# Delta layer of a streaming encoder step: VectorE's scan work moved between its places, transfers issued in the scan, output norms applied on ScalarE

## The chip, the cores and the metric

The kernel runs on one core of one Trainium2 chip. The metric is device time in microseconds (us). Before the change it is 1423.12 us, the median of 3 runs (1422.04 to 1426.44).

## What is computed

One inference step of two layers on 1024 prompt tokens and 8 sample sequences of 16 tokens, model width 1024. Layer 0 (a gated linear recurrence beside window attention) is untouched. Layer 1 is a gated delta rule with 8 heads of 128 channels. For each head, cut to what matters (the kernel works in chunks of 128 tokens, 8 for the prompt, and takes the 8 samples together as a ninth):

```python
v_new = u_i - w_i @ state                       # per chunk i, in order
o_i   = (q_i * exp(g_i)) @ state + qk_i @ v_new
state = state * exp(g_last) + (k_i * exp(g_last - g_i)).T @ v_new
...
o = rms_norm(o, head_norm) * silu(z)
y = o @ w_out
```

Ahead of it q, k and v come from a projection, a causal convolution of four taps, a SiLU and (q, k) an l2 norm.

## The kernel before

The code is written engine by engine; semaphores order the engines, and each engine runs its own list in order. All data are float32.

Layer 1 is a loop over heads `h`. A head has a part `rest` (the inverse of the unit lower triangular matrix of each chunk, made of many 32x32 products in rounds `r`, and the gram matrices) and a part `scan` of eight steps `k`, one for each chunk. Then three last places (`TAIL + 1` to `TAIL + 3`) lead to the next head.

TensorE has two jobs. The chain of the scan is short, and between its products TensorE makes the projection of head `h + 1`. This is cut into 112 matmuls 288 wide, spread by `SLOTS` over numbered places `p`, two to three for each; `fill(h, p, ahead)` issues a place's share. Scan step `k` has the places 12+3k, 13+3k and 14+3k. One step of the scan on TensorE is: two products with the state `SP` (`ks_mm`, which needs `st_ready`, and `qs_mm`, which needs `o_ready`), fill; a product with `RR` (`tr_mm`, which needs `r_ready`), fill; two products with `VN` (`kv_mm`, `o_mm`), fill. A projection uses sums of weight blocks, which GpSimd makes (`head_sums`: three additions of 128x512, then `last_sum`: one), since each pair of column blocks is multiplied in seven half products rather than eight.

VectorE, in each step, makes `RR`, copies `VN`, updates `SP` and adds `OO[:, k]` (one output chunk). `between(h, p, ahead)` gives each place its share of other work for head `h + 1`: the additions of half products (`added_half`), and one convolution tap (`tap`, placed by `TAP`). `exponents` prepares three chunks of the decay matrix `EE` at a time from a row that a DMA broadcasts (`rows`); `silu` finishes a convolved row; `normed` multiplies output chunks by the reciprocal norms `fo`, which GpSimd makes (`norms`); `outputs` then takes their transposes from TensorE. A 128x1024 addition updates the sample states `SS1` in step 5.

ScalarE, in each step, scales `QE`, squares `OO[:, k]`, and does the first taps and the tanh of the SiLU (placed by `TANH`). `exponent` takes the exponential of `EE`.

SyncE issues all DMAs from one queue, in order (`head` in its block): the sample states in (`SS1`) and out, weights (`weights`, 512 KB for each of four column blocks `m`), short histories of the convolution (`history`, three transfers with pieces of 12 bytes), the row for `EE` (`rows`), and the gate row of the head before (`y_dram`). `head_sums(h + 1, 1)` is the first thing in GpSimd's `scan` and needs the weights `m` = 3 and 2 of head `h + 1`; `head_sums(h + 2, 0)` follows `compact`, which needs the exponential.

Of the kernel before, what the change touches and what calls it, by code (L numbers as in the profile page):

```python
# [18 lines left out]
ALU = mybir.AluOpType  # L19
# [144 lines left out]
def closed(p):  # L164
# [9 lines left out]
       24: (QUERY, 0, 1), 25: (QUERY, 0, 2), 26: (QUERY, 0, 3), 27: (QUERY, 1, 1), 28: (QUERY, 1, 2), 29: (QUERY, 1, 3),  # L174
       36: (VALUE, 0, 1), 37: (VALUE, 0, 2), 38: (VALUE, 0, 3)}
LAST_TAP = {0: (VALUE, 1, 1), 1: (VALUE, 1, 2), 2: (VALUE, 1, 3)}
TANH = {25: KEY, 31: QUERY}
# [73 lines left out]
def encoder(nc, I, O):  # L251
    ctx = ExitStack()
    with ctx:  # L253
# [184 lines left out]
        def _(sp):  # L438
# [176 lines left out]
            def head(h, ahead):  # L615
                if h:
                    sp.wait_ge(sem("ss_out"), 16 * h)
                sp.dma_start(SS1, I["gs"][bass.ds(h, 1)].rearrange("a p s v -> p (a s) v")
                             ).then_inc(sem("ss_in"), 16)
                if 1 <= h <= H - 2:  # L620
                    sp.wait_ge(sem("y1_done"), 3 * h)
                    sp.wait_ge(sem("row_kept"), 16 * (h - 1))
                    sp.dma_start(y_dram[h - 1], YT[:, gate_row(h - 1)]).then_inc(sem("row_kept"), 16)
                if not ahead:
                    for k in range(3, KT):
                        if k in (3, 5, 7):
                            sp.wait_ge(sem("s1_ready"), 3 * H + (k - 7) // 2)
                        sp.dma_start(w1out[k], I["wout"][1, :, k]
                                     ).then_inc(sem("wout1_in" if k < KT - 1 else "wout_in"), 16)
                    sp.wait_ge(sem("hist1"), 6 * H)  # L630
                    sp.dma_start(O["cb1"], CB1).then_inc(sem("out1"), 16)
                if ahead:
                    if h:
# [15 lines left out]
                if h == H - 2:  # L649
                    sp.wait_ge(sem("row_kept"), 16 * (H - 2))  # L650
                    for i, step in enumerate(("6", "7", "5")):
                        sp.wait_ge(sem("st_mm"), passed(h + 1, 1, step))
                        for k in (2 * i, 2 * i + 1):
# [3 lines left out]
                             ).then_inc(sem("ss_out"), 16)  # L657
                if h == H - 2:
# [5 lines left out]

            for h in range(H - 2):
# [925 lines left out]
        def _(act):  # L1591
# [333 lines left out]

            def scan(h, ahead):
                for k in range(8):
# [74 lines left out]
        def _(dve):  # L2002
# [532 lines left out]
            def silu(h, m):  # L2535
# [3 lines left out]
                dve.scalar_tensor_tensor(S1[:, m, 0:SEQ], T[:, 0:SEQ], 1.0, CV[:, m, 0:SEQ],  # L2539
                                         ALU.add, ALU.mult)  # L2540
# [65 lines left out]
            def norm_q(h):  # L2606
# [5 lines left out]
                c.sync()  # L2612
# [380 lines left out]
```

## Time and profile before

| | |
|---|---|
| median of 3 runs | 1423.12 us |
| profiled execution, its own time | 1421.56 us |
| its span, first to last instruction | 1419.7 us |
| PE busy | 1367.3 us, 96% |
| DVE busy | 818.0 us, 58% |
| ACT busy | 419.7 us, 30% |
| POOL busy | 262.1 us, 18% |
| mean granted TensorE clock | 0.996 |

PE is TensorE (PEld its weight loads), DVE VectorE, ACT ScalarE, POOL GpSimd, SP SyncE; SPq is SyncE's queue of issues. The times of matmuls overlap, and their ends are modelled, so a busy PE can still lose time between two starts. Idle time is given in brackets with what ended it. L923 is the helper line of all matmuls, L926 of all transposes. A float32 matmul shows as two instructions. Layer 1's heads take the span from about 600 to 1350 us, one head about 90 us; the rows below show mostly the fifth head, whose scan runs from about 1023 to 1067 us. Scan steps take 5 to 6 us each.

### The profile page before, as it was taken

The page shows a single profiled execution, that of the slowest core. Times are in us where ns is not written, and L with a number is a line of the kernel's source. Part 1 is how long each engine was busy: PE and PEld are TensorE (multiplying, and loading weights), DVE is VectorE, ACT ScalarE, POOL GpSimd, SP SyncE. Part 2 cuts the span into 40 slices and gives each one's busy share as a digit, 9 for nine tenths or more (in the row PEclk, how much of TensorE's full clock was granted, in tenths as well). Part 3 has the DMA queues.
Part 4 walks back from the last instruction along what each step waited for, and adds up shares of the span by engine and source line. Part 5 has one row for each costly group of instructions (what it writes and reads, how often), then busy time and mean ns, then how long its engine had stood idle before and what let it go on. Part 6 is the DMA issues. An engine that isn't in the chain of part 4 may idle for free.

```text
span 1419.7 us, 30686 instructions
## 1 busy us (share of the span) xinstructions
PE 1367.3 (96%) x12976; PEld 934.0 (66%) x12976; DVE 818.0 (58%) x1851; ACT 419.7 (30%) x990; POOL 262.1 (18%) x402
## 2 busy tenths in 40 slices
PE   5999999999999999999999999999999999999998
PEld 3577765666653455567777777777778778765543
DVE  3747872444432343775867748658577585772244
ACT  4214441444420322422323223233132331322111
POOL 1113200000000112332412223123231232210111
PEclk9999999999999999999999999999999999999999
DMA  9520107000056301211120211201112111240133
GB/s 370 226 46 28 37 7 318 1 1 1 10 231 229 112 30 60 59 48 19 63 67 30 80 20 50 79 31 51 50 45 72 42 50 50 97 165 2 47 119 118
DMA packets 56316, 112.16 MB, mean 79 GB/s; under 512 B 34698, under 2 KB 37586, under 8 KB 53346
## 3 DMA queue, kind: packets, MB, share of 16 engines
q1 hardware_dynamic: 56180, 110.21, 22.2%
q8 instruction: 102, 1.67, 0.5%
q14 instruction: 34, 0.28, 0.1%
HBM read 91.79 MB, written 18.40 MB: 78 GB/s over the span
## 4 chain that ended last, share of the span: by engine, by line
PE 65%; DVE 3%; issue 2%; ACT 0%; DVEq 0%; POOLq 0%; POOL 0%; ACTq 0%
PE psum L923 63%; PE psum L926 2%; DVE mem L2515 1%; DVE mem L2702 0%; DVE mem L2553 0%; DVE mem L2486 0%; DVE mem L2720 0%; DVE mem L2752 0%; DVE mem L2404 0%; DVE mem L2765 0%; DVE mem L2401 0%; DVE mem L2843 0%; DVE mem L2603 0%; DVEq L253 0%; DVE mem L2744 0%
## 5 line engine op out<-in xcount | busy, mean ns | idle before, releaser
L923 PE MATMUL psum<-mem 32*32 32x32 f32 (+11 forms) x12368 | 1306.7, 290 | 31.6 <-issue 14.0
L923 PEld LDWEIGHTS psum<-mem 32*32 32x32 f32 (+5 forms) x12368 | 865.2, 138 | 437.9 <-issue 236.5
L2515 DVE SCALAR_TENSOR_TENSOR mem<-mem 128x576 f32<-128x576 f32 (+1 forms) x126 | 104.2, 827 | 0.0
L926 PE MATMUL psum<-mem 128*128 128x128 f32 (+1 forms) x608 | 85.7, 278 | 15.1 <-ACT mem L1613 10.7
L926 PEld LDWEIGHTS psum<-mem 128*128 128x128 f32 (+1 forms) x608 | 71.2, 144 | 41.3 <-issue 25.6
L754 POOL TENSOR_SCALAR mem<-mem 128x1 f32<-128x1 f32 x17 | 3.7, 215 | 343.8 <-ACT mem L1756 343.8
L1920 ACT ACTIVATE mem<-mem 128x128 f32<-128x128 f32 x72 | 22.0, 305 | 136.1 <-DVE mem L2752 82.9
L2357 DVE SCALAR_TENSOR_TENSOR mem<-psum,mem 128x1024 f32<-128x1024 f32 x12 | 15.2, 1270 | 60.4 <-POOL mem L756 60.4
L1735 ACT ACTIVATE mem<-mem 128x256 f32<-128x256 f32 x72 | 35.5, 494 | 46.4 <-DVE mem L2317 46.4
L1756 ACT ACTIVATE mem<-psum 128x1024 f32<-128x1024 f32 x12 | 12.3, 1025 | 110.8 <-PE psum L923 109.1
L2057 DVE TENSOR_SCALAR mem<-psum,mem 128x128 f32<-128x128 f32 x64 | 21.1, 402 | 39.1 <-PE psum L926 39.1
L1818 ACT ACTIVATE mem<-mem 128x576 f32<-128x576 f32 (+1 forms) x42 | 32.7, 779 | 28.1 <-DVE mem L2493 28.1
L1808 ACT ACTIVATE mem<-psum 128x288 f32<-128x288 f32 x28 | 11.5, 411 | 98.2 <-PE psum L923 98.2
L2307 DVE CUSTOM_DVE_ANT_0 mem<-psum,mem 128x256 f32<-128x256 f32 x72 | 25.6, 421 | 23.7 <-PE psum L923 23.7
L795 POOL TENSOR_TENSOR mem<-mem 128x512 f32<-128x512 f32 x14 | 15.3, 1091 | 119.7 <-issue 115.2
L821 POOL COPY mem<-mem 128x3 f32<-128x3 f32 x24 | 8.4, 350 | 151.7 <-DVE mem L2473 71.2
L2539 DVE SCALAR_TENSOR_TENSOR mem<-mem 128x1024 f32<-128x1024 f32 x24 | 34.9, 1453 | 1.8 <-ACT mem L1847 1.7
L2720 DVE SCALAR_TENSOR_TENSOR mem<-psum,mem 128x128 f32<-128x128 f32 x56 | 19.4, 347 | 27.1 <-PE psum L923 27.1
L1890 ACT ACTIVATE mem<-psum 128x288 f32<-128x288 f32 x32 | 13.1, 411 | 66.6 <-PE psum L923 66.5
L2731 DVE COPY mem<-psum 128x128 f32<-128x128 f32 x64 | 18.6, 290 | 23.4 <-PE psum L923 23.3
L1847 ACT ACTIVATE mem<-mem 128x1176 f32<-128x1176 f32 x24 | 28.2, 1175 | 7.0 <-DVE mem L2404 4.0
L1930 ACT ACTIVATE mem<-psum,mem 128x128 f32<-128x128 f32 x56 | 20.2, 360 | 33.2 <-PE psum L923 33.2
(242 smaller groups left out, 1175.5 us busy)
## 6 DMA issues: line engine op xcount, KB each, us to landing
mem<-modw SPq DMA_DIRECT2D x12, 2048.0 KB, 13.2
mem<-w SPq DMA_DIRECT2D x44, 512.0 KB, 4.0
mem<-x SPq DMA_DIRECT2D x1, 4608.0 KB, 17.9
x_dram<-mem SPq DMA_DIRECT2D x9, 512.0 KB, 2.6
mem<-row_dram SPq DMA_DIRECT2D x8, 576.0 KB, 4.4
mem<-x_dram SPq DMA_DIRECT2D x9, 512.0 KB, 3.6
mem<-wout SPq DMA_DIRECT2D x4, 1024.0 KB, 8.4
mem<-gs SPq DMA_DIRECT2D x8, 512.0 KB, 3.8
```

The source lines that it names most:

```text
L923: return pe.matmul(*a, **k)
L926: return pe.transpose(out, in_, ident[0:n, 0:n])
L1735: c.mark(act.activation(SS[:, a], SS[:, a], ACT.Exp, scale=HD ** -0.5, bias=nm[:, a:a + 1], accum_out=den[:, a:a + 1]))
L1818: act.activation(CV[:, m, lo:hi], U1[:, m, lo:hi], ACT.Copy, scale=CW[:, 3 * g + ORDER[m], 0:1]).then_inc(sem("pj_ev"), 1)
L1847: act.activation(U1[:, m, PRE:], CV[:, m, 0:UC], ACT.Tanh, scale=0.5).then_inc(sem("th1"), 1)
L1920: x = act.activation(SQJ, OO[:, k], ACT.Square, accum_out=sso[:, k:k + 1])
L1930: act.activation(QE, B(7)[:, 0:P], ACT.Copy, scale=HC[:, 0, k:k + 1]).then_inc(sem("qe_ready"), 1)
L2057: i = dve.tensor_scalar(HT[:, k, bass.ds(t * P, P)], src[k], modT[:, KT + k, 0:1], modT[:, k, 0:1], ALU.mult, ALU.add)
L2307: i = dve.tensor_tensor_reduce(SS[:, n], B(bk)[:, a * 256:(a + 1) * 256], mask, 1.0, -3.0e38, ALU.add, ALU.max, mx[:, n:n + 1])
L2515: x = dve.scalar_tensor_tensor(cvm, U1[:, m, lo + j:hi + j], CW[:, 3 * g + ORDER[m], j:j + 1], cvm, ALU.mult, ALU.add)
L2539: dve.scalar_tensor_tensor(S1[:, m, 0:SEQ], T[:, 0:SEQ], 1.0, CV[:, m, 0:SEQ], ALU.add, ALU.mult)
L2720: dve.scalar_tensor_tensor(RR, at_(6, 0), HC[:, 1, k:k + 1], VB[:, k], ALU.mult, ALU.add).then_inc(sem("r_ready"), 1)
```

## The change

- `TANH` and `TAP`: the tanh of the key row moves from place 25 to 24, of the query row from 31 to 32; two taps of the query row move from places 28 and 29 to 29 and 31.
- The addition to `SS1` moves from step 5 (after `OO`) to step 6 (ahead of `VN`).
- `exponents` run in steps 2, 3 and 4, not in 3, 4 and 5.
- The key row's `silu` is cut in two: columns 0 to 511 in step 5, the rest in step 7.
- `normed` leaves VectorE. ScalarE scales each of the nine chunks of `OO` by its own column of `fo`, with one instruction each: four and one in step 5, four after place `TAIL + 1`.
- SyncE: a head's first transfers wait for the first state of the scan (`st_ready` of 8h + 1). Then come `history`, the weights `m` = 2 and 3, `rows` and the gate row to `y_dram`. Before, the gate row and these weights were issued in `rest` round 1, and `history` and `rows` in its later rounds. The next `SS1` is fetched as soon as the last one has been written out. The last head waits the same way, and sends the last block of the output weights after that wait.

```diff
-       24: (QUERY, 0, 1), 25: (QUERY, 0, 2), 26: (QUERY, 0, 3), 27: (QUERY, 1, 1), 28: (QUERY, 1, 2), 29: (QUERY, 1, 3),
+       24: (QUERY, 0, 1), 25: (QUERY, 0, 2), 26: (QUERY, 0, 3), 27: (QUERY, 1, 1), 29: (QUERY, 1, 2), 31: (QUERY, 1, 3),
...
-TANH = {25: KEY, 31: QUERY}
+TANH = {24: KEY, 32: QUERY}
...
             def head(h, ahead):
-                if h:
-                    sp.wait_ge(sem("ss_out"), 16 * h)
...
-                if 1 <= h <= H - 2:
-                    sp.wait_ge(sem("y1_done"), 3 * h)
-                    sp.wait_ge(sem("row_kept"), 16 * (h - 1))
-                    sp.dma_start(y_dram[h - 1], YT[:, gate_row(h - 1)]).then_inc(sem("row_kept"), 16)
                 if not ahead:
-                    for k in range(3, KT):
+                    for k in range(3, KT - 1):
...
+                sp.wait_ge(sem("st_ready"), 8 * h + 1)
...
                 if ahead:
+                    sp.wait_ge(sem("s1_ready"), 3 * h + 3)
+                    history(h + 1)
                     if h:
                         sp.wait_ge(sem("st_mm"), passed(h, 1, "3"))
                         weights(h + 1, 2)
                     else:
                         sp.wait_ge(sem("pj_mm"), 12)
                     weights(h + 1, 3)
-                    sp.wait_ge(sem("s1_ready"), 3 * h + 3)
-                    history(h + 1)
                     sp.wait_ge(sem("eq_ready"), 3 * h + 3)
                     rows(h + 1)
+                    if h:
+                        sp.wait_ge(sem("y1_done"), 3 * h)
+                        sp.wait_ge(sem("row_kept"), 16 * (h - 1))
+                        sp.dma_start(y_dram[h - 1], YT[:, gate_row(h - 1)]).then_inc(sem("row_kept"), 16)
...
                 sp.dma_start(O["ss"][bass.ds(h, 1)].rearrange("a p s v -> p (a s) v"), SS1
                              ).then_inc(sem("ss_out"), 16)
+                if ahead:
+                    sp.wait_ge(sem("ss_out"), 16 * (h + 1))
+                    states(h + 1)
...
+            def normed(h, n, a, b):
+
+                wait(act, sem("fo_ready"), 3 * h + n + 1)
+                for k in range(a, b):
+                    i = act.activation(OO[:, k], OO[:, k], ACT.Copy, scale=fo[:, k:k + 1])
+                i.then_inc(sem("on_ready"), 1)
...
-                    if k == 5 and ahead:
-                        exponent(h + 1)
+                    if k == 5:
+                        normed(h, 0, 0, 4)
+                        if ahead:
+                            exponent(h + 1)
+                        normed(h, 1, 8, 9)
...
                     between(h, TAIL + p, ahead)
+                    if p == 1:
+                        normed(h, 2, 4, 8)
...
-            def normed(h, n, a, b):
-
-                dve.wait_ge(sem("fo_ready"), 3 * h + n + 1)
-                dve.tensor_tensor(OO[:, a:b], OO[:, a:b], bc(fo[:, a:b], 2, P), ALU.mult
-                                  ).then_inc(sem("on_ready"), 1)
...
+                        if k == 6:
+                            dve.wait_ge(sem("sample_mm"), 4 * h + SAMPLE_MM["kv"])
+                            dve.wait_ge(sem("ss_dec"), h + 1)
+                            ss = SS1.rearrange("p (b s) v -> p b (s v)", b=4)
+                            dve.tensor_tensor(ss, ss, psum[:, 2:6, 0:256], ALU.add).then_inc(sem("sample_dve"), 1)
                     dve.wait_ge(sem("tr_mm"), 8 * h + k + 1)
                     dve.tensor_copy(VN, at_(6, 1)).then_inc(sem("vn_ready"), 1)
...
+                    elif k == 5 and ahead:
+                        silu_front(h + 1, KEY, 0, LW)
                     elif k == 7 and ahead:
-                        silu(h + 1, 0)
+                        silu(h + 1, KEY, LW)
...
-                    elif k == 5:
...
-                        dve.tensor_tensor(ss, ss, psum[:, 2:6, 0:256], ALU.add).then_inc(sem("sample_dve"), 1)
-                        between(h, 14 + 3 * k, ahead)
-                        dve.wait_ge(sem("o_ready"), 8 * h + 4)
-                        normed(h, 0, 0, 4)
-                        dve.wait_ge(sem("sample_dve"), 5 * h + SAMPLE_DVE["o"])
-                        normed(h, 1, 8, 9)
...
-                    if ahead and k in (3, 4, 5):
-                        exponents(h + 1, 3 * (k - 3), 3 * (k - 2))
+                    if ahead and k in (2, 3, 4):
+                        exponents(h + 1, 3 * (k - 2), 3 * (k - 1))
```

## Rows read from the trace of the kernel before

**Rows 1.** The page's first part: busy us (share of the span) xinstructions.

```profile
PE 1367.3 (96%) x12976; PEld 934.0 (66%) x12976; DVE 818.0 (58%) x1851; ACT 419.7 (30%) x990; POOL 262.1 (18%) x402
```

**Rows 2.** TensorE's waits from 690 to 1300 us: total, times, longest.

```profile
PE psum L923 <- issue: 13.4, 11, 2.5
PE psum L923 <- DVE mem L2720: 8.7, 7, 1.2
```

**Rows 3.** Timeline of TensorE, fifth head's scan: start us, us, instructions merged.

```profile
1050.67 6.46 PE L923 MATMUL psum<-mem 128*128 128x288 f32 x31
1058.37 1.95 PE L923 MATMUL psum<-mem 128*128 128x128 f32 x8 [1.24 <-DVE mem L2720]
...
1037.05 0.85 PE L923 MATMUL psum<-mem 128*128 128x288 f32 x5
```

**Rows 4.** Timeline of VectorE, same scan, step 5 and the start of 6.

```profile
1054.13 1.21 DVE L2765 TENSOR_TENSOR mem<-mem,psum 128x1024 f32<-128x1024 f32 x1
...
1056.38 0.88 DVE L2702 TENSOR_TENSOR mem<-mem 128x512 f32<-128x512 f32 x2
1057.19 0.87 DVE L2553 SCALAR_TENSOR_TENSOR mem<-mem 128x128 f32<-128x128 f32 x3
1057.98 0.34 DVE L2720 SCALAR_TENSOR_TENSOR mem<-psum,mem 128x128 f32<-128x128 f32 x1
```

**Rows 5.** Timeline of VectorE, same scan: first state, then step 2.

```profile
1026.17 0.28 DVE L2749 COPY mem<-psum 128x128 f32<-128x128 f32 x1
...
1033.57 0.81 DVE L2515 SCALAR_TENSOR_TENSOR mem<-mem 128x576 f32<-128x576 f32 x1
...
1034.94 0.42 DVE L2736 TENSOR_TENSOR mem<-mem 128x256 f32<-128x256 f32 x1
...
1035.96 0.81 DVE L2515 SCALAR_TENSOR_TENSOR mem<-mem 128x576 f32<-128x576 f32 x1
1036.69 0.34 DVE L2744 SCALAR_TENSOR_TENSOR mem<-mem,psum 128x128 f32<-128x128 f32 x1
...
1037.87 0.34 DVE L2720 SCALAR_TENSOR_TENSOR mem<-psum,mem 128x128 f32<-128x128 f32 x1
```

**Rows 6.** Timeline of VectorE: one SiLU instruction beside GpSimd's addition, one alone.

```profile
1002.85 2.15 DVE L2539 SCALAR_TENSOR_TENSOR mem<-mem 128x1024 f32<-128x1024 f32 x1
...
1067.29 1.22 DVE L2539 SCALAR_TENSOR_TENSOR mem<-mem 128x1024 f32<-128x1024 f32 x1
```

**Rows 7.** Timeline of GpSimd, fifth head.

```profile
1002.83 1.09 POOL L795 TENSOR_TENSOR mem<-mem 128x512 f32<-128x512 f32 x1 [17.51 <-issue]
...
1017.67 1.27 POOL L784 TENSOR_TENSOR mem<-mem 128x512 f32<-128x512 f32 x1 [2.20 <-PE psum L923]
...
1059.38 1.81 POOL L809 COPY mem<-mem 32x288 f32<-32x288 f32 x4 [9.67 <-ACT mem L1852]
```

**Rows 8.** Timeline of SyncE's queue: start and us of the issues.

```profile
1005.23 1.63 SPq L583 DMA_DIRECT2D mem<-cs  x3
...
897.48 0.33 SPq L623 DMA_DIRECT2D y_dram<-mem  x1
```

**Rows 9.** DMA issues from 1083 to 1090 us: KB each, median us to landing.

```profile
mem<-w SPq DMA_DIRECT2D x2, 512.0 KB, 3.6
```

**Rows 10.** Timeline of TensorE in `rest`: stops that no semaphore ended.

```profile
902.42 2.05 PE L923 MATMUL psum<-mem 32*32 32x64 f32 x20 [2.51 <-issue]
...
810.26 1.12 PE L923 MATMUL psum<-mem 128*128 128x288 f32 x2 [1.88 <-issue]
...
1076.59 1.78 PE L923 MATMUL psum<-mem 32*32 32x32 f32 x23 [0.78 <-issue]
```

**Rows 11.** Windows: us, busy us of each engine, PEclk, DMA share, GB/s.

```profile
902.40:905.90 3.50, 3.48 (x24) 2.59 (x24) 1.45 (x5) 0.00 (x0) 0.00 (x0) 0.51 0.02 5
810.30:813.70 3.40, 3.40 (x12) 2.82 (x12) 1.21 (x2) 0.00 (x0) 0.00 (x0) 0.50 0.39 116
```

**Rows 12.** ScalarE scaling 128x128 by a column: ns min/median/max.

```profile
L1943 ACT ACTIVATE mem<-mem x64: 384/389/396, 667.2 to 1308.3; 128x128 f32<-128x128 f32 x64
```

More of the change, by code:

```diff
@@ L613, in _, with states, head @@
                 weights(1, ORDER[i])
-            def head(h, ahead):
-                if h:
-                    sp.wait_ge(sem("ss_out"), 16 * h)
+            def states(h):
                 sp.dma_start(SS1, I["gs"][bass.ds(h, 1)].rearrange("a p s v -> p (a s) v")
                              ).then_inc(sem("ss_in"), 16)
-                if 1 <= h <= H - 2:
-                    sp.wait_ge(sem("y1_done"), 3 * h)
-                    sp.wait_ge(sem("row_kept"), 16 * (h - 1))
-                    sp.dma_start(y_dram[h - 1], YT[:, gate_row(h - 1)]).then_inc(sem("row_kept"), 16)
+            def head(h, ahead):
                 if not ahead:
-                    for k in range(3, KT):
[L626 to L629, printed above, removed]
+                    for k in range(3, KT - 1):
+                        sp.wait_ge(sem("s1_ready"), 3 * H - 2 if k < 5 else 3 * H - 1)
+                        sp.dma_start(w1out[k], I["wout"][1, :, k]).then_inc(sem("wout1_in"), 16)
+                sp.wait_ge(sem("st_ready"), 8 * h + 1)
+                if not ahead:
+                    sp.wait_ge(sem("s1_ready"), 3 * H)
+                    sp.dma_start(w1out[KT - 1], I["wout"][1, :, KT - 1]).then_inc(sem("wout_in"), 16)
                     sp.wait_ge(sem("hist1"), 6 * H)
@@ L663, in head @@
                              ).then_inc(sem("sp_out"), 16)
+            states(0)
             for h in range(H - 2):
@@ L2533, in gated, with silu_front, silu @@
                                          ).then_inc(sem("z_ev"), 1)
-            def silu(h, m):
+            def silu_front(h, m, a, b):
                 dve.wait_ge(sem("th1"), 3 * h + m + 1)
                 T = U1[:, m, PRE:]
-                dve.scalar_tensor_tensor(S1[:, m, 0:SEQ], T[:, 0:SEQ], 1.0, CV[:, m, 0:SEQ],
-                                         ALU.add, ALU.mult)
+                dve.scalar_tensor_tensor(S1[:, m, a:b], T[:, a:b], 1.0, CV[:, m, a:b], ALU.add, ALU.mult)
+            def silu(h, m, a=0):
+                silu_front(h, m, a, SEQ)
                 sm = lambda a: a.rearrange("p (s u) -> p s u", s=NS)[:, :, 0:DS]
@@ L2612, in norm_q @@
                 c.sync()
+                if h:
+                    dve.wait_ge(sem("fo_ready"), 3 * h)
                 c.tell(dve.tensor_scalar(f1, ssq, P * EPS, 4 * P * EPS * EPS, ALU.mult, ALU.add),
@@ L2760, in scan @@
                                                  ALU.mult, ALU.add).then_inc(sem("sample_dve"), 1)
-                    elif k == 5:
-                        dve.wait_ge(sem("sample_mm"), 4 * h + SAMPLE_MM["kv"])
-                        dve.wait_ge(sem("ss_dec"), h + 1)
-                        ss = SS1.rearrange("p (b s) v -> p b (s v)", b=4)
-                        dve.tensor_tensor(ss, ss, psum[:, 2:6, 0:256], ALU.add).then_inc(sem("sample_dve"), 1)
-                        between(h, 14 + 3 * k, ahead)
-                        dve.wait_ge(sem("o_ready"), 8 * h + 4)
-                        normed(h, 0, 0, 4)
-                        dve.wait_ge(sem("sample_dve"), 5 * h + SAMPLE_DVE["o"])
-                        normed(h, 1, 8, 9)
                     elif k == 7 and ahead:
                         silu(h + 1, 1)
-                    if ahead and k in (3, 4, 5):
-                        exponents(h + 1, 3 * (k - 3), 3 * (k - 2))
-                    if k != 5:
-                        between(h, 14 + 3 * k, ahead)
+                    if ahead and k in (2, 3, 4):
+                        exponents(h + 1, 3 * (k - 2), 3 * (k - 1))
+                    between(h, 14 + 3 * k, ahead)
                     if k == 6:
@@ L2789, in head @@
                     between(h, TAIL + 2, ahead)
-                dve.wait_ge(sem("o_ready"), 8 * h + 8)
-                normed(h, 2, 4, 8)
                 if ahead:
```

## The prediction

> **What bounds the kernel now.** I began with the page's busy times: TensorE 96%, VectorE 58% [rows 1]. So TensorE's order of work sets the end, and another engine matters only where it lets TensorE stop. Next came TensorE's waits over the heads [rows 2]. Two rows hold nearly all of it: 8.7 us in 7 waits for VectorE's L2720 (`RR`), and 13.4 us in 11 stops put down to "issue", which no semaphore ended. Nothing else in some 600 us. These 22 us are what the change can win; it takes no work from TensorE.
>
> The seven waits are one for each head that has a next one. TensorE's timeline [rows 3] has the matmuls of step 5 running to 1050.67 + 6.46 = 1057.13, and the first product with `RR` of step 6 at 1058.37: idle for 1.24 us. VectorE's timeline [rows 4] tells why `RR` was late. From 1054.13 to 1058.32 it has no idle time in the rows: the addition to `SS1` (1.21), two taps and additions between, the two `normed` (0.88), three `exponents` (0.87), then `RR`, which ends at 1057.98 + 0.34 = 1058.32.
>
> **VectorE's load in step 5.** After the change the addition to `SS1` (1.21), both `normed` (0.88, on to 1057.19 where the next starts, so 0.81 net) and the `exponents` (0.79 net, 1057.19 to 1057.98) are gone from ahead of `RR`, and one of the taps moves to step 6 (0.81). Half a key row comes in (512 columns; by the 1.22 us of 1024 columns in [rows 6], some 0.6). Together over 3.6 - 0.6 = 3.0 us less against 1.24 us of lateness: the wait goes, with over 1.5 us to spare. **Term 1: 7 x 1.24 = -8.7 us.** Unless something else is in the way this is close to certain. In step 6 the addition of 1.21 stands ahead of the copy of `VN`. `RR` of that step now has ended early, and TensorE works some 1.5 us of fill between the product with `RR` and the one with `VN`; I expect it to just fit, priced with term 3.
>
> **ScalarE's nine columns.** The nearest row is the same operation and form, 128x128 scaled by a column, 389 ns [rows 12]. Four take about 1.6 us at most and nine 3.5 us a head, where VectorE spent 0.88 on five of them. ScalarE is busy 30% [rows 1] and the transposes that need them come a step later; the next `QE` needs them past by then. **Cost 0**, hidden by TensorE's fill of steps 5 and 6. If that cover were gone it would be the 1.6 - 0.7 = 0.9 us that four instructions take more than one. The exponential no longer waits for `RR`'s neighbours, so `compact` on GpSimd starts some 2 us sooner.
>
> **The transfers.** What moves: three `history`, two weights, `rows` and the gate row, seven issues on SyncE's queue, all now behind the first state, which ends at 1026.17 + 0.28 = 1026.45 [rows 5]. Three `history` issues took 1.63 us in `rest`; with the next wait behind them the first weight is issued about 1.8 us later, at 1028.3, the second at 1028.7. A pair of weights alone landed in a median of 3.6 us from its issues, so the second later than that [rows 8, 9]. Some of that is shared with `history` in front. I put the second weight's landing at 1033.3, bounds 1032.5 and 1035. The row for `EE` follows at about 1035, its first reader is `exponents` of step 2 at about 1037: in time, by 2 us.
>
> Who waits for the weights? `head_sums(h + 1, 1)`, the first thing in GpSimd's scan. Before, it ran at 1017.67 in `rest` [rows 7], where VectorE had nothing urgent. Now three additions of 1.27 us each start at about 1033.3 and run to 1037.3.
>
> **That meets VectorE.** At 1002.85 VectorE's SiLU instruction of 1024 columns started 0.02 us after GpSimd's L795, and took 2.15 us. Alone the same one took 1.22 [rows 6, 7]. It is 0.93 longer, nearly the 1.09 that GpSimd's addition took: one ran after the other. So I take it that an instruction of VectorE with two inputs in memory and a GpSimd addition exclude each other. In step 2 VectorE has three such instructions, all with `mem<-mem`: two taps (0.81) and L2736 (0.42), between 1033.57 and 1036.69 [rows 5]. Walk it: the first addition holds 1033.3 to 1034.6, and the tap due at 1033.57 waits 0.9; the second addition gets in behind it, and L2736 waits about 0.7; the third, and the second tap waits about 0.8, with some 0.7 us of this taken up by slack and by work on PSUM between. The state update L2744, before at 1036.69, comes at about 1038.3 and ends at 1038.7. TensorE's products with that state stood at about 1037.3 (the group at 1037.05 is one last 128x288 and then four of 128x128, [rows 3]). A new stop of 1.4 us, and it falls on `ks_mm` in step 3. `RR` then follows at once, since the three `exponents` that moved into step 2 run under TensorE's fill. The first head loads one weight less there: 0.4. **Term 2: 6 x 1.4 + 0.4 = +8.8 us.** Bounds: 0.3 a head if the weights land before 1032 (the last addition alone is in the way), so 2; and 2.0 a head if they land at 1035 (then the additions cut the `exponents` apart), so 12. I take the value of the walk.
>
> **Term 3, step 6.** `compact` ends nearer 1059 than 1061.2 (L809, 1059.38 + 1.81, [rows 7]) and the next `head_sums` then begins beside the moved tap. By the same lock that tap waits about 0.5, and of it some 0.15 reach TensorE; the late `VN` may add as much. 6 x 0.15 = **+0.9 us**, bounds 0 and 4 (the whole 0.5 and some).
>
> **Term 4, the stops in `rest`.** The three "issue" stops that [rows 10] show stand in `rest`, among or behind its small matmuls. With no transfer of data under way one was 0.78 us (1076.59). Two of the largest, 2.51 and 1.88, came with a transfer of the gate row just issued, at 897.48 [rows 8] for the one, and after both the granted clock is 0.5, the lower of its two levels (1.2 of 2.4 GHz) [rows 11], for 3.4 us or so: another 1.7 of lost work each at most. With the weights, history and gate row out of `rest`, I bring those two down to 0.8 (-2.8), the clock back (-2.4, as part of that window is not full of matmuls), and others by little or nothing. **-5 us**, bounds 0 (the stops fall where they fall) and -11 (all that came near a transfer vanish).
>
> The Trainium skill, "Runtime: NRT & Kernel Launch", § Instruction fetch mechanics, says that instructions are fetched by DMA in blocks of 256 and that this is hidden, since the sequencer issues more slowly than the blocks come. By that rule term 4 would be 0 and the time about 1423. The trace does not agree, where small matmuls leave a few ns apart: 13.4 us of stops without a semaphore. That a fetch is what TensorE waits for there is the page's mechanism and my reading; no row shows the cause.
>
> **Sum.** 1421.6 - 8.7 + 8.8 + 0.9 - 5 = 1417.6 in the profiled execution's own time. It stood 1.6 below the median of the runs, and such stops vary; I add half, **1418**, 0.35% below the median. The measurement tells about 0.3% (4.3 us) from no change.
>
> **Rivals.**
> *The lock does not reach TensorE* (the weights land early or late enough, or the taps fall between the additions): term 2 and 3 vanish, 1418 - 9 = 1409. For it: the exact hit depends on half a microsecond, and the slack of 1.24 us waits shows VectorE otherwise in time. Against: three additions back to back cover 4 us, in which VectorE has three instructions of the kind and is busy nearly throughout. 0.22.
> *The stops in `rest` stay*: the change's scan terms cancel, 1423. For it: the stop at 1076.59 without any transfer, and the page's rule. Against: the largest two stand beside transfers. 0.17.
> *Slower, by the lock.* The weights land near 1035 and the stop before the state's products grows to 2 us or more. The point from which it decides is an idle of about 1.9 us: after 1.24 the clock stayed up, after 1.88 and 2.51 it fell [rows 3, 10, 11]. Then each of six heads loses 2.2 + up to 1.7 there in place of 1.4: 1423 - 8.7 + 13 (no clock lost) to 23 (all of it) + 1 - 5, so 1423 to 1433, and with the clock lost in two heads of three 1430. For it: seven transfers go out at once, and I know each only nearly alone. Against: the landing would have to slip 1.7 us. 0.14.
> *The forecast itself*, 0.47, own range 1413 to 1422.
>
> **How the numbers follow.** Faster by over 0.3% is under 1418.9: the first rival (0.22) and rather over half of the forecast (0.29), 0.51. Slower, over 1427.4: three quarters of the slower rival (0.10) and 0.02 of the others' far ends, 0.12. What is left, 0.37, is the same. The range of 8 in 10: 1408 (the first rival's centre, and a microsecond for term 4's good end) to 1427 (half of the slow case inside).
>
> **What the profile after would show.** L2720 gone from TensorE's waits, or few ns: term 1. A new row "PE <- DVE L2744", six times some 1.2 us, before the state products of step 3, L784 to L788 at the same time, and taps L2515 with a maximum near 1.7 us instead of 0.84: term 2. If these are absent the first rival holds. Fewer and shorter "issue" stops, PEclk without the two dips: term 4. I would be wrong at the root if VectorE waited in step 2 for the broadcast row, if `QE` came late behind ScalarE's columns, or if `VN` in step 6 became the new late thing behind the 1.21 us addition.

## The result, and the profile after

The changed kernel takes 1415.24 us, the median of 5 runs (1414.17 to 1418.22); in the same job the kernel before took 1424.82 (1422.04 to 1426.44). The ratio is 0.9937, with a 95% interval of 0.9919 to 0.9955: faster, by 9.6 us, of which the bound of 0.3% asks 4.3. The forecast was 1418, own range 1413 to 1422. The profiled execution has a span of 1413.3 us (before: 1419.7), its own time 1415.07. TensorE's busy time is 2.4 us less than in [rows 1]; the rest of the gain is in how long it stood:

```profile
PE 1364.9 (97%) x12976; PEld 929.3 (66%) x12976; DVE 822.2 (58%) x1834; ACT 439.0 (31%) x1062; POOL 269.5 (19%) x402
```

Lines moved by some 6 to 24. The ones that matter: the matmul helper L923 is L929, `RR` L2720 is L2737, the copy of `VN` L2731 is L2753, `VM` L2736 is L2758, the state update L2744 is L2768, the tap L2515 is L2533, the additions L784 to L788 are L790 to L794. TensorE's waits from 690 to 1300 us, which answer to [rows 2] (total, times, longest):

```profile
PE psum L929 <- issue: 10.0, 12, 1.4
PE psum L929 <- DVE mem L2768: 3.9, 6, 1.0
PE psum L929 <- DVE mem L2737: 1.8, 5, 0.4
PE psum L929 <- DVE mem L2753: 0.2, 1, 0.2
```

The wait for `RR` in step 6 is gone, all seven times (8.7 us). A new stop stands where the state update feeds step 3, in all seven heads (the first head's, 0.39 us at 673.73, lies before this window), followed in five of them by a short one for that step's `RR`. In these rows 5.7 us came back. The stops without a semaphore are 3.4 us less. In the fifth head, TensorE's timeline at that place:

```profile
1025.66 3.04 PE L929 MATMUL psum<-mem 128*128 128x288 f32 x14
...
1029.64 2.17 PE L929 MATMUL psum<-mem 128*128 128x128 f32 x10 [0.94 <-DVE mem L2768]
...
1032.18 20.17 PE L929 MATMUL psum<-mem 128*128 128x128 f32 x106 [0.37 <-DVE mem L2737]
```

The idle time in such rows is less than what a stop costs, as the ends of matmuls are modelled. A surer measure is the time from the start of one matmul to the start of a later one, the same two in every kernel. In each head 336 matmuls stand between a lone transpose ahead of the scan and the five transposes of its step 6. The fifth head before, then after:

```profile
1013.35 43.78 PE L923 MATMUL psum<-mem 32*32 32x32 f32 x324
...
1060.60 0.71 PE L926 MATMUL psum<-mem 128*128 128x128 f32 x5
```

```profile
1004.60 24.10 PE L929 MATMUL psum<-mem 32*32 32x32 f32 x220
...
1052.19 0.71 PE L932 MATMUL psum<-mem 128*128 128x128 f32 x5
```

That is 47.25 us before and 47.59 after. Over the seven heads that have a next one it is 330.7 before and 330.5 after. So in the scan the new stop took back all that the old one gave, and the gain lies outside it. "By starts" means this measure from here on.

VectorE's timeline at the new stop answers to [rows 5], where the tap took 0.81 and L2736 0.42:

```profile
1024.82 0.81 DVE L2533 SCALAR_TENSOR_TENSOR mem<-mem 128x576 f32<-128x576 f32 x1
...
1026.19 1.40 DVE L2758 TENSOR_TENSOR mem<-mem 128x256 f32<-128x256 f32 x1
1027.51 0.44 DVE L2513 TENSOR_TENSOR mem<-mem,psum 128x288 f32<-128x288 f32 x1
1027.88 1.46 DVE L2533 SCALAR_TENSOR_TENSOR mem<-mem 128x576 f32<-128x576 f32 x1
1029.25 0.33 DVE L2768 SCALAR_TENSOR_TENSOR mem<-mem,psum 128x128 f32<-128x128 f32 x1
...
1029.71 1.43 DVE L2574 SCALAR_TENSOR_TENSOR mem<-mem 128x128 f32<-128x128 f32 x3
```

And GpSimd's, which answers to [rows 7]; the first addition waited for its weights:

```profile
1026.04 1.26 POOL L790 TENSOR_TENSOR mem<-mem 128x512 f32<-128x512 f32 x1 [19.34 <-DMA mem<-w]
1027.38 1.33 POOL L792 TENSOR_TENSOR mem<-mem 128x512 f32<-128x512 f32 x1
1028.80 1.67 POOL L794 TENSOR_TENSOR mem<-mem 128x512 f32<-128x512 f32 x1
```

Each of VectorE's instructions with two inputs in memory that meets this stretch takes 0.56 to 0.98 us more than alone. Those with one input in PSUM do not: L2513 took 0.44 in the middle of it, as it does elsewhere.

Why did the additions start at 1026.04? The copy that releases SyncE's transfers, the first state of the scan, is this one in VectorE's timeline:

```profile
1017.42 0.28 DVE L2773 COPY mem<-psum 128x128 f32<-128x128 f32 x1
```

It was done at 1017.70, and GpSimd had the last weight 8.3 us later, where the forecast had 6.85. SyncE's queue shows it:

```profile
1017.73 1.62 SPq L583 DMA_DIRECT2D mem<-cs  x3
1019.40 2.15 SPq L560 DMA_DIRECT2D mem<-w  x2
```

Two weights alone are issued in 0.8; behind three `history` transfers the first issue took 1.68 of the 2.15 here, and 1.81 in the fourth head, but only 0.58 to 0.63 in the other five. With the landing late by this, and DMA shared with all that was issued beside it (4.6 us from issue to landing instead of 3.6, [rows 9]), the weights came 1.5 us later than forecast, inside the bound of 1035 (8.55 us after the state).

### The profile page after: what moved, and what is told of

Read it like the earlier page. It is cut to its first block, busy times and chain, and to the rows that moved or that the text cites. A ratio compares the mean times of both kernels' runs of the same rounds, so it can differ in the third digit from the quotient of the medians.

```text
span 1413.3 us, 30732 instructions
## 1 busy us (share of the span) xinstructions
PE 1364.9 (97%) x12976; PEld 929.3 (66%) x12976; DVE 822.2 (58%) x1834; ACT 439.0 (31%) x1062; POOL 269.5 (19%) x402
## 3 DMA queue, kind: packets, MB, share of 16 engines
q8 instruction: 102, 1.67, 0.5%
## 4 chain that ended last, share of the span: by engine, by line
PE 65%; DVE 4%; issue 2%; ACT 0%; DVEq 0%; POOLq 0%; POOL 0%; ACTq 0%
PE psum L929 62%; PE psum L932 2%; DVE mem L2533 1%; DVE mem L2513 0%; DVE mem L2422 0%; DVE mem L2574 0%; DVE mem L2758 0%; DVE mem L2753 0%; DVE mem L2768 0%; DVE mem L2756 0%; DVE mem L2624 0%; DVE mem L2737 0%; DVE mem L2419 0%; DVE mem L2776 0%; DVE mem L2854 0%
## 5 line engine op out<-in xcount | busy, mean ns | idle before, releaser
L929 PE MATMUL psum<-mem 32*32 32x32 f32 (+11 forms) x12368 | 1304.1, 290 | 27.7 <-issue 10.0
L929 PEld LDWEIGHTS psum<-mem 32*32 32x32 f32 (+5 forms) x12368 | 860.4, 137 | 436.4 <-issue 231.1
L2533 DVE SCALAR_TENSOR_TENSOR mem<-mem 128x576 f32<-128x576 f32 (+1 forms) x126 | 112.3, 891 | 0.0
L790 POOL TENSOR_TENSOR mem<-mem 128x512 f32<-128x512 f32 x14 | 18.6, 1328 | 129.4 <-DMA mem<-w 128.8
L2557 DVE SCALAR_TENSOR_TENSOR mem<-mem 128x1024 f32<-128x1024 f32 (+1 forms) x31 | 35.9, 1158 | 1.9 <-ACT mem L1853 1.8
L801 POOL TENSOR_TENSOR mem<-mem 128x512 f32<-128x512 f32 x14 | 15.2, 1089 | 112.5 <-issue 108.1
L2737 DVE SCALAR_TENSOR_TENSOR mem<-psum,mem 128x128 f32<-128x128 f32 x56 | 19.4, 347 | 25.4 <-PE psum L929 25.4
L2753 DVE COPY mem<-psum 128x128 f32<-128x128 f32 x64 | 18.4, 288 | 20.9 <-PE psum L929 20.9
L2768 DVE SCALAR_TENSOR_TENSOR mem<-mem,psum 128x128 f32<-128x128 f32 x56 | 19.2, 344 | 17.1 <-PE psum L929 17.1
```

The source lines that it names most:

```text
L929: return pe.matmul(*a, **k)
L2533: x = dve.scalar_tensor_tensor(cvm, U1[:, m, lo + j:hi + j], CW[:, 3 * g + ORDER[m], j:j + 1], cvm, ALU.mult, ALU.add)
L2557: dve.scalar_tensor_tensor(S1[:, m, a:b], T[:, a:b], 1.0, CV[:, m, a:b], ALU.add, ALU.mult)
L2737: dve.scalar_tensor_tensor(RR, at_(6, 0), HC[:, 1, k:k + 1], VB[:, k], ALU.mult, ALU.add).then_inc(sem("r_ready"), 1)
L2768: dve.scalar_tensor_tensor(SP, SP, EG[:, bass.ds(h, 1), k], at_(6, 2), ALU.mult, ALU.add).then_inc(sem("st_ready"), 1)
```

## The experiments

Each of e1 to e10 was timed in five rounds (4 to 12 runs) beside the kernel before on the same chip. "Change" is the difference of the two medians. "Idle" is TensorE's, from the profile's waits between 690 and 1300 us: for VectorE, and stops without a semaphore. Before the change these are 8.7 and 13.4. "Scan" is the stretch of 336 matmuls by starts, seven heads together, less the 330.7 of before. "Elsewhere" is the change less "scan"; it sets medians against a single profile, so a microsecond or two of it means little.

| kernel | us | before, us | change | ratio, 95% interval | idle for VectorE | issue stops | scan | elsewhere |
|---|---|---|---|---|---|---|---|---|
| after | 1415.24 | 1424.82 | -9.6 | 0.9937, 0.9919 to 0.9955 | 5.9 | 10.0 | -0.2 | -9.4 |
| e1, weights back in `rest` | 1410.36 | 1423.81 | -13.4 | 0.9916, 0.9904 to 0.9929 | 0 | 14.7 | -10.5 | -3.0 |
| e2, transfers only | 1422.20 | 1423.81 | -1.6 | 0.9988, 0.9977 to 1.0000 | 11.8 | 8.2 | +5.4 | -7.0 |
| e3, work only | 1415.17 | 1423.81 | -8.6 | 0.9944, 0.9926 to 0.9963 | 0 | 18.5 | -10.1 | +1.4 |
| e4, quarter additions | 1409.93 | 1423.81 | -13.9 | 0.9908, 0.9895 to 0.9921 | 0.7 | 12.6 | -9.1 | -4.8 |
| e5, weights first in the scan | 1412.82 | 1424.02 | -11.2 | 0.9922, 0.9905 to 0.9939 | 1.8 | 11.2 | -6.4 | -4.8 |
| e6, e1 and gate row in `rest` | 1416.69 | 1424.02 | -7.3 | 0.9947, 0.9930 to 0.9964 | 0 | 18.2 | -10.5 | +3.2 |
| e7, e1 and history, rows in `rest` | 1411.07 | 1424.02 | -12.9 | 0.9912, 0.9896 to 0.9928 | 0 | 13.0 | -10.5 | -2.5 |
| e8, e1 and norms on VectorE | 1412.34 | 1424.02 | -11.7 | 0.9915, 0.9899 to 0.9930 | 1.1 | 14.3 | -10.5 | -1.2 |
| e9, before, gate row in the scan | 1419.96 | 1423.22 | -3.3 | 0.9975, 0.9960 to 0.9989 | 8.7 | 11.8 | 0.0 | -3.2 |
| e10, e1 and additions held back | 1419.53 | 1423.22 | -3.7 | 0.9973, 0.9961 to 0.9986 | 5.3 | 13.2 | -1.9 | -1.8 |

**e1: the two weights issued in `rest` again, all else as changed.** My theory was that GpSimd's additions, put into step 2 by the late weights, hold VectorE; the rival that VectorE is late there for another reason, its new order.

```
+                if ahead:
+                    if h:
+                        sp.wait_ge(sem("st_mm"), passed(h, 1, "3"))
+                        weights(h + 1, 2)
+                    else:
+                        sp.wait_ge(sem("pj_mm"), 12)
+                    weights(h + 1, 3)
                 sp.wait_ge(sem("st_ready"), 8 * h + 1)
...
                     history(h + 1)
-                    if h:
-                        sp.wait_ge(sem("st_mm"), passed(h, 1, "3"))
-                        weights(h + 1, 2)
-                    else:
-                        sp.wait_ge(sem("pj_mm"), 12)
-                    weights(h + 1, 3)
                     sp.wait_ge(sem("eq_ready"), 3 * h + 3)
```

> The kernel after, with one thing put back: the weights of column blocks 2 and 3 are issued in rest again, all other transfers stay in the scan. Theory (VectorE and GpSimd exclude each other): the sums of GpSimd run in rest again, TensorE's waits for the state update (L2768, 3.9 us in 6) and for RR in step 3 (L2737, 1.8 us in 5) go, under 1 us left in all; 6 to 8 us faster than the kernel after by starts of matmuls, less 1 to 2 us of longer stops in rest: about 1410 us, ratio to before 0.990. Rival (the transfers in the scan make the scan late, whatever GpSimd does): history, the row and the gate row are still there, so over half of the waits stay and the time is 1413 to 1415.

1410.36 us. The additions are back in `rest` (1007.31 in the fifth head) and the waits of TensorE in the profile of e1 hold one row:

```profile
PE psum L930 <- issue: 14.7, 13, 3.0
```

VectorE's timeline, step 2 of the same head: nothing is stretched.

```profile
1023.21 0.81 DVE L2534 SCALAR_TENSOR_TENSOR mem<-mem 128x576 f32<-128x576 f32 x1
...
1024.58 0.42 DVE L2759 TENSOR_TENSOR mem<-mem 128x256 f32<-128x256 f32 x1
...
1025.60 0.81 DVE L2534 SCALAR_TENSOR_TENSOR mem<-mem 128x576 f32<-128x576 f32 x1
1026.33 0.34 DVE L2769 SCALAR_TENSOR_TENSOR mem<-mem,psum 128x128 f32<-128x128 f32 x1
```

The changed order of VectorE needs no stop; the place of the weights makes it. By starts the stretch is down to 45.75 us in this head, and 10.2 us shorter than after in the seven. The time is only 3.9 us better than the whole change, each against its own runs of before: the other 6 us are lost outside the scan (see e6 and e7). The two ratios' intervals overlap, and the two were timed in different jobs, so that e1 beats the change is likely rather than shown; every run of e1 (at most 1412.28) lies under every run of the change (at least 1414.17).

**e2 and e3: the two halves of the change.** e2 is the kernel before with SyncE's new order only; e3 the changed kernel with SyncE's old order. e3's edit, cut (e2's is its mirror):

```
+                if 1 <= h <= H - 2:
+                    sp.dma_start(y_dram[h - 1], YT[:, gate_row(h - 1)]).then_inc(sem("row_kept"), 16)
...
-                sp.wait_ge(sem("st_ready"), 8 * h + 1)
...
-                    sp.wait_ge(sem("s1_ready"), 3 * h + 3)
-                    history(h + 1)
                     weights(h + 1, 3)
+                    sp.wait_ge(sem("s1_ready"), 3 * h + 3)
+                    history(h + 1)
```

> The kernel before, with the new order of transfers alone; VectorE and ScalarE as before. Theory: the wait for RR in step 6 stays (8.7 us in 7), a wait for the state update in step 3 comes to it (5 us or so in 6), the stops in rest get 4 to 5 us shorter with the clock's two dips gone: within 3 us of before, ratio 0.998 to 1.002. Rival (transfers and stops have nothing to do with each other): 5 to 6 us slower than before, ratio 1.004.

> The kernel after, with the transfers issued in the old order and places. Theory: no wait for RR in step 6, no wait for the state update in step 3 (the sums of GpSimd run in rest), stops in rest as before the change (13 us or so): 9 to 10 us faster than before, 1415 us, ratio 0.993, the same as the whole change. Rival (stops independent of transfers): the scan's gain of nearly 10 us and no loss in rest against the kernel after, 1409 us, ratio 0.989.

e2's waits of TensorE (`RR` is its L2726, the state update L2750):

```profile
PE psum L929 <- DVE mem L2726: 8.7, 7, 1.2
PE psum L929 <- issue: 8.2, 8, 2.2
PE psum L929 <- DVE mem L2750: 3.1, 6, 0.8
```

The old wait is there in full, the new one too (3.1), and the stops fell from 13.4 to 8.2: what the transfers give at one place they take at the other, -1.6 us, hardly more than the interval tells from nothing. e3 has no wait for VectorE and 18.5 us of stops in 14 (13 or so expected), and gives -8.6. So term 1 belongs to the work alone and term 4 to the transfers alone. Term 2 needs both for its full size: by starts the late transfers alone cost 5.4 us in the scan (e2), and 10.2 with the work in its new places (after against e1). The short wait for `RR` of step 3, behind the `exponents` that moved into step 2, is only in the second.

**e4: the additions a quarter as wide.** It leaves out three quarters of GpSimd's sums for the second pair of weights, and moves nothing. If the additions' time is what VectorE loses, the stop goes though the weights are as late as in the change; if it is the DMA writing into memory then, it stays.

```
+                e = 1 if q else HALF
-                pool.tensor_tensor(SD3, w1[:, 0:HALF], w2[:, 0:HALF], ALU.subtract).then_inc(sem("s_made"), 1)
+                pool.tensor_tensor(SD3[:, 0:e], w1[:, 0:e], w2[:, 0:e], ALU.subtract).then_inc(sem("s_made"), 1)
...
```

> The kernel after, with the three additions of head_sums for the second pair of column blocks cut from 128x512 to 128x128 each (three quarters of these sums are left out, the transfers and waits are all there). Theory (exclusion between the engines): each addition holds some 0.35 us, the waits for L2768 and L2737 in step 3 fall under 1 us in all: 1407 to 1410 us, ratio 0.988 to 0.990. Rival (transfers do it): 1415 us as the kernel after, L2758 and the taps still stretched.

1409.93 us. GpSimd's addition in its timeline, and what is left of TensorE's waits:

```profile
1021.80 0.46 POOL L791 TENSOR_TENSOR mem<-mem 128x128 f32<-128x128 f32 x1 [19.05 <-DMA mem<-w]
```

```profile
PE psum L930 <- issue: 12.6, 11, 2.6
PE psum L930 <- DVE mem L2738: 0.7, 1, 0.7
```

The new stop is gone from all heads but for one wait of 0.7 for `RR` (by starts 1.4 us are left of the 10.2, in two heads), and the time is e1's, though the weights come in the scan.

**e10: e1 with the additions held back to step 2 by a semaphore, no transfer moved.** The mirror of e4.

```
                 if ahead:
+                    wait(pool, sem("r_ready"), 7 * h + 2)
                     head_sums(h + 1, 1)
```

> The kernel with the weights in rest (1410.4 us), where GpSimd now holds its three full additions for the second pair until VectorE has made RR of step 2. The weights landed long before, so no transfer differs from that kernel. Theory (exclusion): the additions meet the taps and L2758 as in the kernel after, the waits of TensorE for L2768 and L2737 come back with 4 to 8 us in all: 1415 to 1418 us. Rival (late transfers were the cause): no waits, 1410.5 us.

1419.53 us. The stop is back: GpSimd's timeline, then VectorE's and TensorE's, in the profile of e10.

```profile
1025.94 1.27 POOL L791 TENSOR_TENSOR mem<-mem 128x512 f32<-128x512 f32 x1 [17.51 <-DVE mem L2739]
```

```profile
1026.54 1.29 DVE L2535 SCALAR_TENSOR_TENSOR mem<-mem 128x576 f32<-128x576 f32 x1
...
1028.26 0.98 DVE L2760 TENSOR_TENSOR mem<-mem 128x256 f32<-128x256 f32 x1
...
1029.53 1.46 DVE L2535 SCALAR_TENSOR_TENSOR mem<-mem 128x576 f32<-128x576 f32 x1
```

```profile
PE psum L931 <- DVE mem L2770: 5.3, 6, 0.9
```

With late transfers and small additions there is no stop; with early transfers and late additions it is there. The lock between GpSimd's additions and VectorE's two-input instructions is shown. The time is 9.2 us over e1 (9.8 by the differences to before), more than the 5.3 of the row, and I had expected at most 1418. By starts it is accounted for: the stretch is 1.2 us longer than e1's in each of the seven heads, 8.6 together. A stop that the row puts at 0.88 or 0.89 us costs 1.2, and the first head's lies before the row's window.

**e5: the two weights ahead of `history` in the scan.** One line of order.

```
                 if ahead:
-                    sp.wait_ge(sem("s1_ready"), 3 * h + 3)
-                    history(h + 1)
...
                     weights(h + 1, 3)
+                    sp.wait_ge(sem("s1_ready"), 3 * h + 3)
+                    history(h + 1)
```

> The kernel after, all transfers still in the scan, but the two weights issued ahead of history. They then land some 4 us after the first state instead of 8.2, and GpSimd's three additions start some 4 us sooner, in step 1, where VectorE has one instruction of the kind. Theory (the moment of the meeting decides): the last addition at most delays the first tap; waits for L2768 and L2737 fall from 5.7 to under 2 us: about 1410 us, as with the weights in rest. Rival (any place in the scan costs the same): 1415 us, the waits move to steps 1 and 2.

The additions start 6.3 us after the first state, where it was 8.3 in the change and some 4 had been expected, so they still end in step 2, beside its second tap. TensorE's waits for VectorE fall from 5.9 to 1.8 us, and by starts the cost in the scan falls from 10.2 to 4.1: the queue's order alone sets how much of them lands on the tight stretch. In time it is 1.6 us better than the change, within the intervals of both, and short of the 1410 expected.

**e6, e7 and e9: which transfer lengthens the stops in `rest`.** e6 and e7 start from e1 and put one group back into `rest`, e9 starts from before and takes the gate row alone out.

In e6, ahead of the weights and of the wait for "st_ready":

```
+                    if h:
+                        sp.wait_ge(sem("y1_done"), 3 * h)
+                        sp.wait_ge(sem("row_kept"), 16 * (h - 1))
+                        sp.dma_start(y_dram[h - 1], YT[:, gate_row(h - 1)]).then_inc(sem("row_kept"), 16)
```

In e7, behind the weights and ahead of that wait:

```
+                    sp.wait_ge(sem("s1_ready"), 3 * h + 3)
+                    history(h + 1)
                     sp.wait_ge(sem("eq_ready"), 3 * h + 3)
                     rows(h + 1)
```

In e9, in the kernel before, behind `rows(h + 1)` instead of behind the state's load:

```
+                    if h:
+                        sp.wait_ge(sem("st_ready"), 8 * h + 1)
...
+                        sp.dma_start(y_dram[h - 1], YT[:, gate_row(h - 1)]).then_inc(sem("row_kept"), 16)
```

> The kernel with the weights in rest (1410.4 us), with the gate row's transfer back in rest too. Scan waits stay at nil. If the stops grow because this 576 KB write stands in front of TensorE's instruction fetch: 2 to 4 us slower, 1413. If history and the row were the cause: 1410.5.

> The kernel with the weights in rest (1410.4 us), with history and the row for EE back in rest. If the short pieces and the row make the stops: 2 to 4 us slower, 1413. If it was the gate row: 1410.5. Scan waits nil in both.

> The kernel before, with one change: the gate row's transfer leaves round 1 of rest and is issued in the scan, after the first state. Theory (this 576 KB transfer lengthens the stops of the gram and inverse matmuls by near 1 us each where it is still moving): the wait for RR in step 6 stays at 8.7 us in 7, the stops shrink; 3 to 5 us faster than before, ratio 0.9965 to 0.998. Rival (it only counts when all transfers are gone from there): no difference, 1.000.

e7 equals e1: `history` and the row for `EE` cost nothing in `rest` that shows. e6 costs 6.1 us against e1 by the differences to before, and 5.6 against e7 beside which it ran, more than the 2 to 4 expected, and brings its stops to 18.2, near the 18.5 of e3. e9 gains 3.3 on before, with `RR`'s 8.7 us still in it. So the write of the gate row to DRAM (576 KB) lengthens the stops. One point of the program in TensorE's timeline, the 368 small matmuls in `rest` that are [rows 10]'s first group, with the gate row in the scan (e1) and then in `rest` (e6):

```profile
894.04 15.06 PE L930 MATMUL psum<-mem 32*32 32x64 f32 x368 [1.02 <-issue]
```

```profile
894.65 15.06 PE L930 MATMUL psum<-mem 32*32 32x64 f32 x368 [2.12 <-issue]
```

In e6 the gate row was issued at 889.71, some 3 us before this stop began, and the pair of weights at 896.33, after it. The stop is there in both: the write makes it longer, it does not make it. At this point the three kernels that write the gate row in `rest` (before, e3, e6) stop for 2.12 to 2.51 us, the nine others for 1.02 to 1.69. In e6 four stops grow against e1, one a head: from none to 1.37, 1.02 to 2.12, 1.23 to 2.05 and 1.69 to 2.24.

The weights are not free in `rest` either. "Elsewhere" is -9.4 to -4.8 in the four kernels that issue them in the scan (after, e2, e4, e5), and -3.2 to -1.2 in the five that issue them in `rest` and the gate row in the scan (e1, e7, e8, e9, e10). Two stops say where some of it goes. All eight kernels with these weights in `rest` stop at one matmul of the second head (0.81 to 1.50 us) and at one of the third (0.62 to 1.78); the four others stop at neither. The third head's place in e1, and the same matmuls in after:

```profile
802.71 8.38 PE L930 MATMUL psum<-mem 128*128 128x128 f32 x275
812.60 8.78 PE L930 MATMUL psum<-mem 32*32 32x64 f32 x221 [1.50 <-issue]
```

```profile
807.17 14.05 PE L929 MATMUL psum<-mem 128*128 128x288 f32 x348 [0.54 <-issue]
```

What is TensorE waiting for there? The traces hold it, on a DMA queue that the program does not issue to. From the page of before:

```profile
q8 instruction: 102, 1.67, 0.5%
```

These are 102 packets of 16 KB. TensorE has 25952 instructions (12976 matmuls of two each), about 254 for each packet. From 600 us on the twelve profiles have 144 stops of TensorE without a semaphore, and every one ended 1.2 to 1.6 us after such a packet had ended. They fall on 17 places of TensorE's list, and these lie a whole number of times 126.5 matmuls (253 instructions) apart, to within 4. In after, the DMAs from 893.0 to 895.7 us, around the stop from 894.68 to 895.70, are one packet, from 893.12 to 894.24:

```profile
DMA packets 1, 0.02 MB, mean 6 GB/s; under 512 B 0, under 2 KB 0, under 8 KB 0
...
q8 instruction: 1, 0.02, 2.6%
```

So the stops are waits for TensorE's next block of instructions. What the gate row does can be read at the point above: the block starts 4.4 us after the one before it in e1, 5.9 in e6 and 6.2 in before, and takes no longer itself (1.31, 0.93 and 0.95 us). The write makes the block start late. No run changed the fetching itself, and why a write holds it back is open.

**e8: the nine norms on VectorE again, on top of e1.** Could the spread of the other work have done without ScalarE's columns?

From ScalarE's program, in three places, the first of them:

```
-                        normed(h, 0, 0, 4)
```

and back in VectorE's:

```
+                dve.wait_ge(sem("fo_ready"), 3 * h + n + 1)
+                dve.tensor_tensor(OO[:, a:b], OO[:, a:b], bc(fo[:, a:b], 2, P), ALU.mult
+                                  ).then_inc(sem("on_ready"), 1)
```

> The kernel with the weights in rest (1410.4 us), with normed on VectorE again, in its old places. By the prediction's working VectorE had over 1.5 us to spare in step 5, and normed takes 0.81 of it: no wait for RR comes back, 1410 to 1411 us. Rival (ScalarE's columns are what took the wait away): L2720's wait returns with 0.4 us or more a head, 1413 us or more.

It could. 1412.34 us, and no wait for `RR`; TensorE has six waits of 0.2 for a state update where e1 has none, but by starts the stretch is as long as e1's (45.75 us a head). The intervals of the two ratios cover each other.

## Why the prediction was right

**Term 1, -8.7: right, and worth more.** The seven waits are gone, in e3 too, where the transfers stayed as they were (no wait for VectorE left, -8.6 us). By starts the stretch falls from 47.25 to 45.75 us where nothing comes in its place (e1), 10.5 us in seven heads: a stop that the rows put at 1.24 cost 1.4 to 1.5. VectorE's step 5 has slack enough to take the norms back (e8).

**ScalarE's columns, 0: right.** No engine waits for them in the profile after. Four columns take 1.26 us, less than the 1.6 allowed:

```profile
1047.64 1.26 ACT L1936 ACTIVATE mem<-mem 128x128 f32<-128x128 f32 x4
```

**Term 2, +8.8: the mechanism right, the size near.** By starts it is 10.2 us (after against e1): 1.1 in the first head, where 0.4 was forecast, and 1.3 to 1.8 in the six others, where it was 1.4. The rows of idle time show only 5.7 (3.9 at L2768, 1.8 at `RR` right behind it) and would make the term look too large. In the fifth head, which the walk described, it is 1.84 by starts and 0.94 + 0.37 = 1.31 in the rows. The walk's particulars were off. The weights landed 1.5 us later than it had them, so the first tap escaped, and `VM` took nearly all of the first addition (+0.98), the second tap the next (+0.65), the `exponents` the last (+0.56). That `RR` does not "follow at once" is this last one: the `exponents` that moved into step 2 stand ahead of it. One head's landing was taken for all; the second weight landed 7.0 to 8.2 us after the first state in the six heads. That so different a walk gives nearly the same sum is luck.

The Trainium skill, "GPSIMD Engine Reference", § Specifications, says that GpSimd shares its memory interfaces with VectorE, with contention for VectorE's instructions with two inputs in SBUF. This case agrees, with +0.98 us on an instruction of 0.42; the page gives no price.

**Term 3, +0.9: right about the lock, nearly nothing for TensorE.** The moved tap did meet GpSimd's additions in step 6, by VectorE's timeline of the profile after:

```profile
1052.68 1.20 DVE L2533 SCALAR_TENSOR_TENSOR mem<-mem 128x600 f32<-128x600 f32 x1
```

That is 0.36 more than its 0.84, and no stop for it follows. By starts the matmuls of step 6 take as long as in e1, to 0.01 us a head. The one wait of 0.2 for the copy of `VN` belongs to term 2: it stands in the third head, just before the state's stop.

**Term 4, -5: right in place and near in size.** Stops 13.4 to 10.0 us, -3.4 (2.8 forecast). The two stretches at the lower clock level are gone, too: the 368 matmuls that took 16.69 us in before behind a stop of 2.51 (the granted clock 0.51 of full speed just behind it, [rows 11], so the level of 1.2 GHz) take 15.06 after, at full clock:

```profile
895.70 15.06 PE L929 MATMUL psum<-mem 32*32 32x64 f32 x368 [1.02 <-issue]
```

```profile
895.00:912.00 17.00, 16.30 (x376) 14.01 (x376) 10.71 (x18) 3.29 (x6) 1.09 (x1) 1.00 0.01 3
```

That is 1.63 for this one and 1.65 for the other (127 matmuls, 7.19 us in before and 5.54 at the same point of e6), 3.3 where 2.4 was forecast; with the stops -6.7. By starts all that lies outside the scan's stretch is 6.2 us shorter than before. Of the transfers that I named together, the gate row's write and the weights have a share, and `history` has none that shows.

Rival "the stops stay" is out. With it goes the page's rule: "Runtime: NRT & Kernel Launch" of the Trainium skill, § Instruction fetch mechanics, holds that fetching is hidden. This case does not agree: the stops that no semaphore ended are 10.0 us even now, each behind a packet of the instruction queue. The prediction's "no row shows the cause" was true of the rows that it took; the page of before had this queue.

**The sum.** By starts: -10.5 (term 1), +10.2 (term 2), 0 (term 3) and -6.2 elsewhere (term 4) make -6.4 us with their roundings, the whole difference between the two profiled spans. The forecast for the profiled execution was -4.0. Terms 1 and 2 were both too small, by 1.8 and 1.4, since both were counted in idle time as the rows give it; that these errors cancel is luck. Term 3 was 0.9 too large and term 4 1.2 too small. The medians differ by 9.6 and not by 6.4 because the profiled execution of before (1421.56) ran 3.3 us under the median of its runs and that of after (1415.07) at its own.

The slower rival had its landing (8.2 us after the state, near its 8.55), but not its stop: the largest was 1.31 us over two waits, 1.84 by starts, and the clock stayed up. Its point of about 1.9 us for the clock does not hold. In before itself a stop of 2.32 us ended at 1255.50, and the granted clock behind it was full; in e1 it fell to 0.57, behind a stop of 1.69 us that ended at 1072.08:

```profile
1255.40:1259.00 3.60, 3.50 (x72) 2.94 (x73) 1.62 (x4) 0.48 (x1) 0.00 (x0) 1.00 0.79 319
```

```profile
1073.00:1077.00 4.00, 4.00 (x20) 3.16 (x14) 2.23 (x5) 0.00 (x0) 0.00 (x0) 0.57 0.24 76
```

## What to carry to other kernels

When a transfer is moved, follow it to the first instruction that its landing releases, and look at what other engine is tight at that moment: here three GpSimd additions of 1.3 us that cost nothing in one stage cost TensorE 1.1 to 1.8 us a head in the next. Measure a stop by the starts of the same two matmuls in both kernels: idle time in the rows gave 5.7 us for what cost 10.2. Of a change with several parts the halves should be timed apart; here one gave -8.6 us and the other -1.6, and taking back one piece of the second (the weights) gave -13.4. Taking a write to DRAM out from under a stretch of very small matmuls gave 3.3 us at no cost (e9). The weights' loads cost there too, but in the scan, as the change had them, they cost more.

## What the runs showed of the hardware

- A GpSimd addition of 128x512 and a VectorE instruction with two inputs in memory exclude each other for nearly their whole length: 0.42 became 1.40, 0.81 became 1.46, three of 0.87 became 1.43, and GpSimd's 1.27 became 1.67. VectorE's instructions with one input in PSUM were as fast as ever (0.44).
- The issue of a transfer behind three `history` transfers on SyncE's queue took 1.68 and 1.81 us in two of after's seven heads and 1.99 in e1's fifth, instead of 0.6; they bring 12 KB each, and in the window of these issues 3152 of 3480 packets were under 512 B. Small pieces can cost the transfers behind them.
- TensorE's instructions come in blocks of 16 KB, one for each 253 or so. Where they are short (32x32 matmuls) it stops for a block, at much the same points of the program in every kernel (0.2 to 3.3 us each, 8 to 18 us in all). It starts again 1.2 to 1.6 us after the block's packet has ended. A 576 KB write to DRAM ahead of one made 1.02 into 2.12, and costs 3.3 us (e9) to 6.1 us (e6) over the kernel.
- Open: why the write holds a block back; how much of the time "elsewhere" the weights in `rest` cost (2 to 6 us by the medians); and what besides the length of a stop decides whether the clock falls.
